# Gated delta rule: block inverses solved outside the scan by substitution on DVE, and a scan over 32x32-blocked inverses

## What is computed

```python
m = strict_lower(einsum(k * beta, k) * decay)          # per chunk
sol = triangular_solve(m + I, concat[v * beta, k * beta * exp(gc)])
u, w = sol[..., :dv], sol[..., dv:]
attn = einsum(q, k) * decay
def step(state, (qd, kd, uu, ww, at, cd)):             # chunk after chunk
    v_new = uu - ww @ state
    o = qd @ state + at @ v_new
    state = state * cd + kd.T @ v_new
out = concat([rmsnorm(ret) * silu(rg), rmsnorm(gdn) * silu(gg)]) @ w_out
```

## Time and profile before

| | |
|---|---|
| median of 3 runs | 3010.96 us (3009.13 to 3011.68) |
| the profiled execution | 3011.53 us, its span 3009.6 us |
| TensorE busy | 2871.6 us, 95% of the span |
| DVE busy | 1695.8 us, 56% |
| ACT busy | 880.0 us, 29% |
| POOL busy | 391.5 us, 13% |
| mean granted clock of TensorE | 0.968 |

### The profile page before, as it was taken

The page is one execution under the profiler, slowest core; times in us unless marked ns, Lnnn a source line. Parts: engine busy times, 40 slices in busy tenths (PEclk is TensorE's granted clock), DMA queues, the critical chain, the costliest instruction groups (busy, mean ns, idle before and its releaser), DMA issues.

```text
span 3009.6 us, 50197 instructions
## 1 busy us (share of the span) xinstructions
PE 2871.6 (95%) x19829; PEld 2769.0 (92%) x19829; DVE 1695.8 (56%) x2599; ACT 880.0 (29%) x1203; POOL 391.5 (13%) x321
## 2 busy tenths in 40 slices
PE   5999999999789899999999999999997999999998
PEld 3999999998488889999999999999994779999998
DVE  3687776446555545697776563533627766323225
ACT  4222123333211124412122522112523655212123
POOL 1000002100133243000001200000301543000002
PEclk7999999999799989999999999999987999999999
DMA  7354453321100003454453332322320003232323
GB/s 241 120 173 148 140 153 127 99 62 66 48 1 1 0 8 94 138 161 140 150 158 126 106 119 70 126 70 84 126 71 4 1 16 112 70 84 70 84 70 105
DMA packets 331886, 281.27 MB, mean 93 GB/s; under 512 B 9836, under 2 KB 292584, under 8 KB 331752
## 3 DMA queue, kind: packets, MB, share of 16 engines
q1 hardware_dynamic: 331752, 279.42, 30.4%
HBM read 275.72 MB, written 3.67 MB: 93 GB/s over the span
## 4 chain that ended last, share of the span: by engine, by line
PE 82%; DVE 7%; issue 4%; ACT 3%; POOL 2%; DVEq 0%; DMA 0%; SPq 0%; POOLq 0%; ACTq 0%
PE ps L316 67%; PE ps L1522 2%; PE ps L1534 2%; PE ps L1532 2%; PE ps L827 1%; DVE w_lo L297 1%; PE ps L1868 1%; PE ps L1881 1%; POOL sq_acc L476 1%; PE ps L1858 1%; ACT w_hi L290 1%; PE ps L854 1%; POOL h_raw L516 1%; PE ps L1859 1%; DVE mod_acc L372 1%
## 5 line engine op out<-in xcount | busy, mean ns | idle before, releaser
L316 PE MATMUL ps<-h_hi,w_hi 128*128 128x320 f32 x3712 | 1152.7, 311 | 13.9 <-DVE h_lo L543 5.0
L316 PE MATMUL ps<-h_lo,w_hi 128*128 128x320 f32 x3712 | 1148.8, 309 | 0.0
L316 PE MATMUL ps<-h_hi,w_lo 128*128 128x320 f32 x3712 | 1148.7, 309 | 0.0
L316 PEld LDWEIGHTS ps<-h_hi,w_hi 128*128 128x128 f32 x3712 | 698.4, 188 | 20.8 <-issue 14.0
L316 PEld LDWEIGHTS ps<-h_lo,w_hi 128*128 128x128 f32 x3712 | 698.5, 188 | 0.2
L316 PEld LDWEIGHTS ps<-h_hi,w_lo 128*128 128x128 f32 x3712 | 698.4, 188 | 0.0
L290 ACT CAST w_hi<-w_raw 128x2048 fp32r<-128x2048 f32 x188 | 357.9, 1904 | 640.6 <-PE ps L316 622.9
L297 DVE TENSOR_TENSOR w_lo<-w_raw,w_hi 128x2048 fp32r<-128x2048 f32 x188 | 433.3, 2305 | 124.6 <-ACT w_hi L290 124.6
L316 PE MATMUL ps<-hid_hi,w_hi 128*128 128x320 f32 x1408 | 437.0, 310 | 0.0
L316 PE MATMUL ps<-hid_hi,w_lo 128*128 128x320 f32 x1408 | 435.1, 309 | 0.0
L316 PE MATMUL ps<-hid_lo,w_hi 128*128 128x320 f32 x1408 | 435.0, 309 | 0.0
(11 more groups left out here) (254 smaller groups left out, 2719.9 us busy)
## 6 DMA issues: line engine op xcount, KB each, us to landing
w_raw<-in_ffn_w_in_dram SPq DMA_DIRECT2D x176, 512.0 KB, 5.2
mod_raw<-in_mod_w_dram SPq DMA_DIRECT2D x64, 1024.0 KB, 5.2
w_raw<-in_ffn_w_out_dram SPq DMA_DIRECT2D x96, 512.0 KB, 4.4
w_raw<-in_even_w_in_dram SPq DMA_DIRECT2D x28, 512.0 KB, 4.3
w_raw<-in_ffn_w_out_dram SPq DMA_DIRECT2D x32, 384.0 KB, 5.4
mod_first<-in_mod_w_dram SPq DMA_DIRECT2D x4, 2048.0 KB, 18.9
w_raw<-in_even_w_out_dram SPq DMA_DIRECT2D x16, 512.0 KB, 4.0
w_raw<-in_odd_w_out_dram SPq DMA_DIRECT2D x16, 512.0 KB, 4.2
```

The costliest lines, as they stand in the source:

```text
L316: mm = nc.tensor.matmul(ps[:, 4 * s + 2 * n + b, 0:HALF], w[s][:, k, cols], v[:, k, b * HALF:(b + 1) * HALF], start=(first and k == 0), st ...
```

## The change

The inversion leaves the round. After the input projection, `pe_prep`, `act_prep` and `dve_prep` make the matrices of all five tiles and both directions at once, into `gn`: slot 0 minus the strictly triangular matrix (its decay with beta folded in by a bias of the exponential, `e_bias`, and the mask as a second matmul that adds a large negative `far`), slot 1 the attention matrix. The 32x32 diagonal blocks (5 tiles x 4 heads x 2 directions x 4 blocks) go through DRAM into `blocks`, one matrix pair a partition, 80 partitions; DVE inverts them by forward substitution, 30 steps of a product and a sum, spread over units 2 to 9 of retention; they go back through DRAM into `gn` and `xa`, `xs`. The levels 32 and 64 of the doubling stay, as small matmuls (`pe_level`, four parts for each step), put one step ahead between the large matmuls of the scan. The scan is token-major: state and output have tokens or keys on the partitions, so the norm of the delta rule's output is a row sum; the keys are turned once (`pe_k_turn`). Three of five tiles are normed while the scan ends. The mask constants and their load go. The weights of `even_out` are loaded late, since their place holds `gn`. The norm by matmul is left for the four retention tiles.

The core of the diff:

```diff
-        for name, tiles, blocks, scale in (("even_out", [4, 5, 6, 7, 0, 1, 2, 3], 1, 1.0 / RDV),
+        for name, tiles, blocks, scale in (("even_out", [4, 5, 6, 7], 1, 1.0 / RDV),
...
-            sp_linear(sp, "even_out", ins["even_w_out"][0], 4)
...
+            sp_blocks_in(sp)
             sp.wait_ge(sr_out, 2)
...
+            sp_blocks_back(sp)
...
+            sp.wait_ge(oo_mm, 4)
+            sp_linear(sp, "even_out", ins["even_w_out"][0], 4)
             sp_linear(sp, "even_out", ins["even_w_out"][0], 4, sweep=1)
...
+                if m >= 2:
+                    dve_solve_steps(dve, SOLVE_AT[m - 2], SOLVE_AT[m - 1])
...
+        def pe_prep(pe):
...
+            for i, n in enumerate(PREP_TILES):
                 for d in range(2):
...
+                    for h in range(GH):
+                        o = ps[:, 4 + v % 4, h * P:(h + 1) * P]
+                        nc.tensor.matmul(o, g_tok[:, n, GH * d + h:GH * d + h + 1].to_broadcast([P, P]), tri[:, d, :], start=True, stop=False)
+                        mm = nc.tensor.matmul(o, ident[:, :], far[:, d, :], start=False, stop=True)
...
+        def sp_blocks_in(sp):
+
+            sp.wait_ge(prep_out, 20)
+            for d in range(2):
+                for b in range(4):
+                    r = slice(32 * b, 32 * b + 32)
+                    sp.dma_start(scr_n[d, r, :].rearrange("r (m c) -> r m c", c=32), gn[r, :, 0, d, r]).then_inc(scr_in, 16)
+            sp.wait_ge(scr_in, 128)
+            for d in range(2):
+                for b in range(4):
+                    sp.dma_start(blocks[20 * b:20 * b + 20, d, :, :],
+                                 scr_n[d, 32 * b:32 * b + 32, :].rearrange("r (m c) -> m r c", c=32)).then_inc(scr_in, 16)
...
+        def dve_solve_steps(dve, k0, k1):
...
+            for k in range(k0, k1):
+                rows, cols = 31 - k, k
...
+                nc.vector.tensor_tensor(part, two_slots(b, *col, [[32, rows], [0, cols]]), two_slots(b, *row, [[0, rows], [1, cols]]),
+                                        ALU.mult).then_inc(sub_mul, 1)
+                dve.wait_ge(sub_mul, k)
+                o = two_slots(b, *out, [[32, rows], [1, cols]])
+                nc.vector.tensor_tensor(o, o, part, ALU.add).then_inc(sub_add, 1)
...
+        def pe_level(pe, t, part):
...
+                    if part == 0:
+                        for a, b in pairs(d):
+                            mm = nc.tensor.matmul(ps[blk(b), 6, 32 * h:32 * h + 32], gn[blk(a), m, 0, d, blk(b)], inverse_of(d, a, m),
+                                                  start=True, stop=True)
...
+        def pe_scan(pe):
+            for part in range(4):
+                pe_level(pe, 0, part)
+            for t in range(5):
...
+                    for h in range(GH):
+                        mm = nc.tensor.matmul(ps[:, 3 * d, h * P:(h + 1) * P], keys(n, h), gs[d][:, h, :], start=True, stop=True)
...
+                pe_level(pe, t + 1, 0)
```

More of the change, by code:

```diff
@@ new lines, in dve_solve_end, with act_blocks_turn @@
+        def dve_solve_end(dve):
+            b = blocks[:, :, :, :]
+            dve.wait_ge(sub_add, 30)
+            nc.vector.memset(bass.AP(b.tensor, 0, [[2048, 80], [1024, 2], [33, 32]]), 1.0).then_inc(sub_add, 1)
+        def act_blocks_turn(act):
+            act.wait_ge(sub_add, 31)
+            act.wait_ge(o_out, RH)
+            for d in range(2):
+                t = nc.scalar.copy(blocks_t[:, d, :, :], blocks[:, d, :, :].rearrange("p r c -> p c r"))
+            t.then_inc(yt_ready, 1)
@@ L1638, in pe_even @@
             pe_qk_spread(pe, 3)
+            pe_prep(pe)
             pe_values(pe)
             pe_ret(pe)
-            pe_gdn(pe)
-            for d in range(2):
-                gdn_wait(pe, "o_added", d, 5)
+            pe_k_turn(pe)
             pe_tnorm_sums(pe, "even_out")
             pe_tnorm_spread(pe, "even_out", 3)
-            pe.wait_ge(tn_out, 16)
+            pe.wait_ge(tn_out, 12)
+            pe_scan(pe)
             pe_linear_out(pe, "even_out", (mo_lo, 0))
```

769 lines of the change are left out of this document (449 added, 320 removed).

## The result

The median after is 2806.5 us (four runs, 2805.9 to 2808.0) against 3011.0 (four runs, 3009.1 to 3011.7): a ratio of 0.9322, 95% interval 0.9310 to 0.9334. The profiled execution took 2806.7 us, its span 2804.9.

The account below looks back on a forecast made before the run. The prediction took the delta rule to be bound by TensorE in lockstep with its helpers. Its new time line put the output projection at 971 instead of 1144.2, gaining 173 us: 3011 - 173 = 2838 us, range 2808 to 2900.

Parts of the forecast that it names:

- (1), (2): After the input projection: copy and spread to 752 us, then preparation of all five tiles, 26.7 us on TensorE, ready at 781.
- (3): Diagonal blocks' trip out and back through DRAM before the substitution: 18 us at 20 ns a piece, to 799.
- (4): Substitution between retention units: 32.6 us of DVE work, bounds 29 to 53; DVE bounds retention, ending at 843.
- (5): Solved blocks' return through DRAM, to 867, beside the retention heads' norm, to 868; scan starts at 869.
- (6): Scan's level 0 at 9 us, step 0 at 12, steps 1 to 3 at 16.6 each; small matmuls 0.12 us each.
- (7): Last scan step and tail, bound by DVE: 30 us, output projection as if begun 23 us after 940, at 963.
- (8): TensorE's clock in the scan, between the delta rule's 0.92 and the patchy stages' 0.70 and 0.68: 8 us added.
- A: Rival for the DRAM transfers: small pieces cost 60 ns instead of 20, 48 us more, 2886 us; chance 0.14.
- D: Rival, slower than before: DMA pieces not spread over the queue's engines; two engines cancel the gain, one gives 3198; chance 0.04.
- the prediction's last rival: The substitution is left exposed after retention: 21 us more, inside the range; no chance of its own given.
- B: Rival: the scan runs at TensorE's lower clock, 54 us more less the 8 counted, 2884 us; chance 0.12.
- C: Rival, all cheaper: pieces at 13 ns, small matmuls at 0.06 us, no clock loss, 2805 us; chance 0.08.

Follow-up runs that it names:

- e1: Changed kernel with every small matmul issued four times, whole sets repeated so neighbours lie on different tiles of TensorE's array: 2845.7 us.
- e2: Changed kernel with every small matmul issued four times, ordered so that all on one tile of the array stand side by side: 2923.9 us.
- e11: Changed kernel with each small matmul once, but those on the same tile of the array side by side, four in a row: 2817.2 us.
- e15: Changed kernel with only the last head's 14 of a level's 56 small matmuls made, so the output is wrong: 2803.7 us.
- e12: Changed kernel with only the first of the 30 substitution steps made, transfers kept, so the output is wrong: 2789.0 us.
- e13: Changed kernel with VectorE's tail reordered: two sums of squares after its additions, three low parts after the late tokens' normalisation: 2803.6 us.
- e6: Changed kernel with the two copies that turn the solved blocks made by VectorE, directly behind the substitution, instead of ScalarE: 2803.4 us.

## Why the prediction missed, step by step

On the prediction's own time line (its 971 against 939.8):

| step | forecast | measured | adds |
|---|---|---|---|
| start | 749.0 | 747.3 | -1.7 |
| (1), (2) copy to first store | 32 | 781.3 - 747.3 = 34.0 | +2.0 |
| (3) blocks out and in | 18 | 795.3 - 781.3 = 14.0 | -4.0 |
| (4) substitution and retention | 44 | 835.75 - 795.3 = 40.4 | -3.6 |
| (5) to the scan | 26 | 860.5 - 835.75 = 24.8 | -1.2 |
| (6) level 0, steps 0 to 3 | 71 | 913.65 - 860.5 = 53.1 | -17.9 |
| (7) tail | 23 | 939.8 - 913.65 = 26.1 | +3.1 |
| (8) clock | 8 | within the above | -8.0 |

They add up to -31.3, all of the miss. The start is no part of the change's mechanism that a run shows: in the runs of the experiments it lies at 746.0 to 748.8. **The step that failed is (6), through the price of the small matmuls**: 0.12 us each, "next to the 64-column row, as a pair of weight load and matmul has to be issued twice whatever its size". The runs put 0.018 for a 32x32 and 0.06 for a 64x64 in its place (e1), shown to hang on the order over the tiles (e2, e11), and 0.021 of time for each of the 42 left out (e15). A level of 56 costs 2.25 us in the changed kernel and not 6.7. Steps 1 to 3 took 12.3 us each for 16.6, which makes 12.9 of the 17.9, the price being 4.45 per step with 0.15 more of waits against it; level 0 and step 0 give 2.6 and 2.1, and rounding the rest. Five levels at 4.45 less would be 22 us; the lower clock of level 0 and step 0 and longer hand-overs in level 0 took some 4 back. I reasoned from the price of matmuls on the whole array; the rows held nothing of tiles in turn, so 0.06 as lower bound was a guess, and for the 32x32 it was too high. The 64-column row was also misread: 0.133 is the mean of a group that began at half clock (granted 0.53 from 2253.2 to 2258.0 us). Its last 150 records, at 1.00, start within 8.1 us, which makes 0.11 per matmul. That is a small part of the error: even at 0.11 a level would have cost 6.2 us.

**(8) was counted on top.** The rows behind it were true: the granted clock is 0.81 in level 0 and 0.78 in step 0, 0.64 before. But the 8 us stood for the whole scan, and steps 1 to 3 run at 1.00. The cost is what level 0 and step 0 pay, by an estimate from the rows some 2.5 us (3.78 for 2.05 us in the first large group, 1.12 for 0.68 in the 64x64 product before it, a little in the 32x32 ones), inside their rows. So part of the miss of (8), over 5 us, is its own and not that of (6).

**(3) and (4) were right in kind, high in size.** The pieces are not dear (A falls) nor bound to one or two engines (D falls). From the first gather's issue to the first substitution it is 6.94 us; the 5120 pieces would take 19.2 at 60 ns on 16 engines, and 51 at 20 ns on two. SP's 5.42 us of issue for eight stores and 4.96 for eight gathers, with 1.65 and 1.98 us to the landing behind them, fill the 14.0. The ten-engine rule that the prediction takes from the Trainium skill ("DMA: Bandwidth & Descriptors", section "Why a DMA increments its semaphore by 16 and not by 1") is neither shown nor excluded: no row here tells ten engines at under 14 ns a piece from sixteen at under 22. The first substitution waits 2.04 us for a DMA. The 60 operations are busy 30.0 us (14.96 + 15.03 in the groups L1464 and L1468), where the prediction's 32.6 less its 2.7 of gaps makes 29.9; so the strided blocks don't halve the rate. e12 confirms 17.5 us exposed, for the 21 of the prediction's last rival.

**(5)** held: the norm's last product at 859.60, not a DMA, releases the scan, as the 868 against 867 had it, though the transfers were done well before: the last was issued by 853.7, and these land after 2.2 us. **(7)** was 3 us short, through the waits on GpSimd's squares and the low parts ahead of the late tokens (e13).

**The rivals.** B, the scan at the lower clock, didn't come, at 0.94 over the scan; e2 shows how it could have. C, "all cheaper", 2805, is closest to what happened: the small matmuls were cheaper than it said, the pieces and the clock in part. It had a chance of 0.08, and I set the low end 3 us above it. That its 2805 lies so near the measured 2806.5 is in part luck: its -17 for the matmuls was some -22, its -8 for the pieces some -5 with all else in (3) and (5), its -8 for the clock some -5.5, and the other steps add up to the rest. With three terms all priced at the middle of wide bounds, the case that all fall to one side deserved its place in the range; that, and not the forecast alone, is why the range missed.

## What to carry to other kernels

Many small matmuls are a cost of TensorE's order before they are one of its count: in turn over the array's tiles 32x32 products cost 0.02 us, four to sixteen in a row on one tile 0.05 to 0.06, and with the second order the clock was lower too in e2 and in the first step of e11. When half of a long dependent chain is to hide beside other work of the same engine, price the sum on that engine, and mix the two; put last, it cost 16.8 us more, part of it because it then met GpSimd's work. A gain at the start of a phase is only a gain if what that phase eats next is ready too: 5.0 us in the tail became 2.9.

## What I had not expected of the hardware

- The granted clock fell to 0.50 with TensorE busy in every record, in stretches of 32x32 matmuls on one tile (e2), and was 1.00 in the kernel's own steps with the same matmuls spread over tiles and 128x128 ones between. It was 1.00 too in steps 1 to 3 of e11, with four in a row on one tile. Why it fell isn't shown.
- In e1, groups of 96 small matmuls in a row, spread over tiles, came with 21 us of waits for issue over the five levels; groups of 64 had none. Why isn't shown.
- VectorE and GpSimd with operands in SBUF held each other up: 1.6 us for each of VectorE's operations beside GpSimd's of 1.61, 0.43 after them.
- A copy of 80x1024 whose read steps over 32 elements took ScalarE 1.95 us and VectorE 2.17, where the prediction had 1.05 for ScalarE from rows without such steps and e6's expectation 1.2 for VectorE.
